# Expert weights in long runs and column halves, scan blocks taken in turn, norm tables loaded once

## The reference, cut to what matters

```python
def expert_block(args):
    xb, e = args
    return (jax.nn.silu(xb @ w_gate[e]) * (xb @ w_up[e])) @ w_down[e]

def _wkv_step(S, inp):
    r_t, w_t, k_t, v_t, a_t, b_t = inp
    sa = jnp.einsum('zbhvk,zbhk->zbhv', S, a_t)
    S = S * w_t[..., None, :] + sa[..., :, None] * b_t[..., None, :] + v_t[..., :, None] * k_t[..., None, :]
    return S, jnp.einsum('zbhvk,zbhk->zbhv', S, r_t)
```

## Time and profile before

| | us |
|---|---|
| median of 3 runs (4897.2 to 4904.73) | 4901.6 |
| span of the profiled execution | 4899.6 |
| expert stage of layer 1 / layer 2 of the second model (32 experts each), to the last down product | 729 / about 729 |
| scan, eight rounds | 1372 |
| TensorE busy | 4236.2 (86%) |
| VectorE busy | 1338.8 (27%) |
| mean granted TensorE clock | 0.789 |

### The profile page before, as it was taken

How to read it: one execution, slowest core, us unless ns; L and a number is a source line. 1 busy time by engine, 2 the same in 40 slices (tenths; PEclk the granted TensorE clock), 3 DMA queues, 4 the chain that set the end, 5 groups by cost and what they waited for, 6 DMA issues and landing times. The chain is left out here.

```text
span 4899.6 us, 68797 instructions
## 1 busy us (share of the span) xinstructions
PE 4236.2 (86%) x28873; PEld 3247.8 (66%) x28873; DVE 1338.8 (27%) x2979; ACT 474.8 (10%) x844; POOL 351.2 (7%) x471
## 2 busy tenths in 40 slices
PE   7996699989993999998497888898898885999996
PEld 6774368875542777776244776786687774777775
DVE  4533635414104000000423333423433322000001
ACT  1002210011001000000101101110110100000001
POOL 0000000000001000000001021112102100000000
PEclk9978569889695899999697555555555556999998
DMA  6732027612112899998110000000000013999995
GB/s 220 232 115 71 1 70 251 203 51 87 35 60 66 256 306 307 307 307 288 52 58 12 1 1 1 2 1 1 2 1 1 1 62 109 300 309 304 311 304 171
DMA packets 547008, 641.48 MB, mean 131 GB/s; under 512 B 26905, under 2 KB 442185, under 8 KB 546425
## 3 DMA queue, kind: packets, MB, share of 16 engines
q1 hardware_dynamic: 507460, 543.65, 34.8%
q10 hardware_dynamic: 31926, 71.73, 4.0%
q0 software_dynamic: 7424, 23.12, 1.7%
HBM read 611.67 MB, written 26.77 MB: 130 GB/s over the span
## 5 line engine op out<-in xcount | busy, mean ns | idle before, releaser
L1560 PEld LDWEIGHTS bank<-ex_xt,weights 128*128 128x128 f32 x8192 | 945.6, 196 | 52.6 <-issue 52.6
L1560 PE MATMUL bank<-ex_xt,weights 128*128 128x64 f32 x8192 | 954.4, 280 | 1.9 <-DVE ex_xt L1612 1.9
L1575 PE MATMUL bank<-weights,ex_hidden 128*64 128x512 f32 x1024 | 457.6, 600 | 4.3 <-DVE ex_hidden L1617 1.4
L394 PE MATMUL bank<-u,weights 128*128 128x272 f32 (+1 forms) x1408 | 318.0, 389 | 16.6 <-DVEq L415 16.6
L1575 PEld LDWEIGHTS bank<-weights,ex_hidden 128*64 128x64 f32 x1024 | 136.0, 138 | 278.3 <-issue 265.2
L394 PEld LDWEIGHTS bank<-u,weights 128*128 128x128 f32 x1408 | 270.3, 192 | 64.3 <-DVEq L415 17.4
L1617 DVE TENSOR_TENSOR ex_hidden<-ex_silu,bank 128x128 f32<-128x128 f32 x128 | 36.8, 288 | 906.8 <-ACT ex_silu L1593 906.8
L2333 PE MATMUL bank<-sc_xt,sc_bt 64*64 64x64 f32 x2560 | 259.4, 314 | 0.0
L2333 PEld LDWEIGHTS bank<-sc_x,sc_n 64*64 64x64 f32 x2560 | 231.9, 220 | 37.4 <-issue 37.4
L2333 PEld LDWEIGHTS bank<-sc_xt,sc_bt 64*64 64x64 f32 x2560 | 245.9, 220 | 0.0
L2333 PE MATMUL bank<-sc_x,sc_n 64*64 64x64 f32 x2560 | 239.4, 314 | 1.0 <-PEq L2253 1.0
(11 more groups left out here) (499 smaller groups left out, 4628.8 us busy)
## 6 DMA issues: line engine op xcount, KB each, us to landing
weights<-in_moe_w_gate_dram SPq DMA_DIRECT2D x128, 1024.0 KB, 5.4
weights<-in_moe_w_up_dram SPq DMA_DIRECT2D x128, 1024.0 KB, 8.0
weights<-in_moe_w_down_dram SPq DMA_DIRECT2D x128, 1024.0 KB, 8.1
ada_w<-in_ada_w_dram ACTq DMA_DIRECT2D x24, 2048.0 KB, 8.7
weights<-in_w_gate_dram SPq DMA_DIRECT2D x22, 1024.0 KB, 5.8
weights<-in_w_up_dram SPq DMA_DIRECT2D x22, 1024.0 KB, 8.2
weights<-in_w_down_dram SPq DMA_DIRECT2D x32, 704.0 KB, 6.7
weights<-in_ga_w_in_dram SPq DMA_DIRECT2D x16, 1024.0 KB, 5.6
```

The costliest lines, as they stand in the source:

```text
L394: last = nc.tensor.matmul(k.bank[b + side * NB][:, 0:N], w[:, f, c * P:(c + 1) * P], rhs[:, f, 0:N], start=(f == 0), stop=(f == DC - 1))
L1560: last = nc.tensor.matmul(k.bank[2 + q][:, o:o + SLOTS], w[:, f * 256 + c * P:f * 256 + (c + 1) * P], xt[:, s, f * SLOTS:(f + 1) * SLOTS], ...
L1575: last = nc.tensor.matmul(k.bank[4 + 2 * s + n][0:SLOTS, :], hid[:, s, f * SLOTS:(f + 1) * SLOTS], w[:, f * 512:(f + 1) * 512], start=(f = ...
```

## The change

- **Experts.** A ring of 18 slots of 1 MB (`ExpertRing`) holds three experts. SP starts the first 18 loads in the route stage. Gate and up rows are now read as "(p k)", 8 KB in one run for each partition, down rows 4 KB. For gate and up the 64 tokens are stationary and 256 columns of the weights move. The two halves of the 512 hidden columns go to partitions 0 to 63 and 64 to 127 of the same bank, so they use the left and the right half of the array. The hidden rows are then turned by two transposes and emptied by VectorE, and down uses the two halves of the array in the same way.
- **Route.** The weights' loads follow the router's small loads on SP's queue. The token rows are stored by ScalarE's queue. The overflow rows are cleared in the attention stage instead (one memset on POOL, three transfers on SP).
- **Scan.** `blocks_matmul` takes the halves in turn. Both halves of the turned copies are products with the identity, and ScalarE empties them. VectorE forms the first level of the inverse right behind each matrix.
- **Modulation.** For the first model's first layer the sums are issued behind the products of four norm stages; the head norms of the second attention are moved ahead of them. The second layer keeps `finish`.
- **Norms.** One table with both functions is asked for ahead of Ln.
- **Gate products of SwiGLU.** The eight chunks are added last to first.
- The first weights of the recurrence are loaded when expert 30 is done, no longer behind the last expert's slots.

```diff
@@ class ExpertRing @@
+    PIECES = 6
+    SLOTS = 18
+    def start(self, sp, a, l, e, j):
+        s = (self.PIECES * e + j) % self.SLOTS
+        if j < 4:
+            w = a["moe_w_gate_2" if j % 2 == 0 else "moe_w_up_2"][l, e]
+            src = w.rearrange("(p k) m -> p (k m)", k=DC)[:, (j // 2) * 2048:(j // 2) * 2048 + 2048]
+            sp.dma_start(self.slots[s], src).then_inc(self.landed[s], 16)
+        else:
+            w = a["moe_w_down_2"][l, e]
+            src = w.rearrange("(k p) m -> p k m", p=P)[:, (j - 4) * 2:(j - 4) * 2 + 2, :]
...
@@ norm_stage, and in the same way head_norm_stage, Prepare.act, scan_output @@
+            nc.scalar.preload_act_table_set("natural_log_exp_and_others")
...
+            if mods is not None:
+                mods.sums(10)
@@ gate_up_stage @@
-                        for f in range(DC):
+                        for f in reversed(range(DC)):
@@ attention_stage @@
+            pool.memset(zero[:, :], 0.0).then_inc(zeroed, 1)
...
+                    sp.dma_start(rows[n], zero[:, 0:width]).then_inc(cleared, 16)
@@ route_stage @@
-            for b in range(nov):
-                sp.dma_start(out_rows[(NE + b) * SLOTS:(NE + b + 1) * SLOTS, :], zero_row[:, :]).then_inc(cleared, 16)
+            for e in range(3):
+                for j in range(k.ring.PIECES):
+                    k.ring.start(sp, a, l, e, j)
@@ experts_stage, TensorE @@
+                    for q in range(4):
+                        f = 4 * j + q
+                        for side in range(2):
+                            w = ring.slot(e, 2 * j + side)
+                            for t in range(2):
+                                last = nc.tensor.matmul(half_cols(k.bank[2 + side], t),
                                                         xt[:, s, f * SLOTS:(f + 1) * SLOTS],
+                                                        w[:, q * 512 + t * 256:q * 512 + t * 256 + 256],
                                                         start=(f == 0), stop=(f == DC - 1))
                     last.then_inc(spent, 1)
+                if e + 1 < NE:
+                    turn(e + 1)
+                pe.wait_ge(gated, e + 1)
+                for c in range(2):
+                    last = nc.tensor.transpose(k.bank[4][:, c * P:(c + 1) * P], hid[:, s, c * P:(c + 1) * P],
+                                               k.ident[:, :])
+                last.then_inc(hturned, 1)
+                pe.wait_ge(hcopied, e + 1)
...
+                    for q in range(2):
+                        o = q * P + j * RH
+                        for n in range(2):
+                            last = nc.tensor.matmul(k.bank[6 + s][n * RH:(n + 1) * RH, :], ht[:, s, o:o + SLOTS],
+                                                    w[:, q * D + n * 512:q * D + n * 512 + 512],
+                                                    start=(j == 0 and q == 0), stop=(j == 1 and q == 1))
@@ scan_matrices @@
-                            if h == 0:
-                                last = nc.tensor.transpose(to, src, k.ident[rows, rows])
-                            else:
-
-                                last = nc.tensor.matmul(to, src, k.ident[rows, rows], start=True, stop=True)
+                            last = nc.tensor.matmul(to, src, k.ident[rows, rows], start=True, stop=True)
...
+                if kind in ("n", "nt"):
+                    x = q.x if kind == "n" else q.xt
+                    dve.wait_ge(masked, n + 1)
+                    nc.vector.tensor_tensor(chunked(x[:, z, :]), chunked(dst[:, z, :]), mask_of(q, M_LEVEL), ALU.mult)\
+                        .then_inc(vinit, 1)
+                    dve.wait_ge(vinit, n + 1)
+                    nc.vector.tensor_tensor(chunked(x[:, z, :]), chunked(x[:, z, :]), mask_of(q, M_ID), ALU.add)
+        @block.scalar
+        def _(act):
+            for n, (kind, z, ops, dst, mask) in enumerate(jobs):
+                if mask is None:
+                    act.wait_ge(made, n + 1)
+                    nc.scalar.activation(dst[:, :] if kind == "vt" else dst[:, z, :], k.bank[n % 4][:, :], ACT.Copy)\
+                        .then_inc(copied, 1)
@@ blocks_matmul @@
-    for h in HALVES:
-        rows = slice(h, h + RH)
-        for j in range(NCH):
-            t = slice(j * CH, (j + 1) * CH)
+    for j in range(NCH):
+        t = slice(j * CH, (j + 1) * CH)
+        for h in HALVES:
+            rows = slice(h, h + RH)
             last = nc.tensor.matmul(ps[rows, t], lhsT[rows, t], rhs[rows, t], start=True, stop=True)
```

More of the change, by code:

```diff
@@ L968, in share, with sums @@
         self.add(dve, r, b * self.ROUND // of, (b + 1) * self.ROUND // of)
-    def finish(self):
+    def sums(self, count):
+        nc = self.k.nc
+        for m in range(self.columns, self.columns + count):
+            for v in range(2):
+                last = nc.tensor.matmul(self.k.bank[7][:, 2 * m + v:2 * m + v + 1],
+                                        self.acc[:, v, m * P:(m + 1) * P], self.k.ones[:, 0:1], start=True, stop=True)
+        self.columns += count
+        last.then_inc(self.summed, 1)
+        self.parts += 1
@@ L1009, in ffn @@
                      side=side)
-        side.finish()
+    return side
 def param(k, name, n=1, at=0):
@@ L1571, in expert @@
-                for n in range(2):
-                    k.stream.wait(pe, seg, e, 4 + n)
-                    w = k.stream.slot(seg, 4 + n)
-                    for f in range(4):
-                        last = nc.tensor.matmul(k.bank[4 + 2 * s + n][0:SLOTS, :], hid[:, s, f * SLOTS:(f + 1) * SLOTS],
-                                                w[:, f * 512:(f + 1) * 512], start=(f == 0), stop=(f == 3))
+                if e + 1 < NE:
+                    turn(e + 1)
+                pe.wait_ge(gated, e + 1)
@@ L1602, in _, with copy @@
-            pairs(act, expert)
-            for s in range(2):
-                act.wait_ge(put[s], 16 * (NE // 2) + 16)
+            def copy(e):
+                act.wait_ge(turned, e + 1)
+                nc.scalar.activation(xt[:, e % 2, :], k.bank[e % 2][:, :], ACT.Copy).then_inc(copied, 1)
+            copy(0)
+            for e in range(NE):
+                s = e % 2
+                act.wait_ge(spent, 4 * e + 2)
+                nc.scalar.activation(act_out[:, s, :], k.bank[2][:, 0:256], ACT.Silu).then_inc(silued, 1)
+                if e + 1 < NE:
+                    copy(e + 1)
+                act.wait_ge(kept, e + 1)
+                for n in range(2):
+                    act.dma_start(out_rows[e * SLOTS:(e + 1) * SLOTS, n * 512:(n + 1) * 512],
+                                  y[n * RH:(n + 1) * RH, s, :]).then_inc(put[s], 16)
@@ L1626, in _ @@
-            copy(0, 0, 0)
-            pairs(dve, expert)
+            for e in range(NE):
+                s = e % 2
+                dve.wait_ge(silued, e + 1)
+                nc.vector.tensor_tensor(hid[:, s, :], act_out[:, s, :], k.bank[3][:, 0:256], ALU.mult)\
+                    .then_inc(gated, 1)
+                dve.wait_ge(hturned, e + 1)
+                nc.vector.tensor_copy(ht[:, s, :], k.bank[4][:, 0:256]).then_inc(hcopied, 1)
+                dve.wait_ge(spent, 4 * e + 4)
+                if e >= 2:
+                    dve.wait_ge(put[s], 32 * (e // 2))
+                nc.vector.tensor_copy(y[:, s, :], k.bank[6 + s][:, :]).then_inc(kept, 1)
@@ L1840, in moe @@
     overflow_stage(k, l, nov, rows, slots, tab, out_rows)
+    more.close()
     combine_stage(k, l, T, desti, wts, out_rows)
@@ L1947, in rwkv @@
         lw, la = sb("lw", [P, TB]), sb("la", [P, TB])
-        k.stream.hold = seg["wo"].first
         r, kx, v = (sb(n, [P, DC, TB]) for n in ("r", "k", "v"))
@@ L2252, in scan_matrices @@
     jobs.append(("vt", 0, (q.v, None), q.vt, None))
+    plain = lambda n: jobs[n][4] is None
+    turned = lambda n: sum(plain(m) for m in range(n + 1))
     with nc.Block() as block:
```

306 lines of the change are left out of this document (149 added, 157 removed).

## The result

The kernel after takes 3983.9 us (median of four runs, 3959.0 to 3994.3) against 4903.1 for the kernel before in the same job: ratio 0.8118, 95% interval 0.8092 to 0.8144. Five more runs in a later job gave 3975.6 (3966.2 to 3991.7). The forecast was 3975. The profiled run took 3987.9 us, its span is 3985.8.

A forecast was written before the change was run, and what follows sets the result against it. TensorE was taken to bound the scan and experts, with transfers close behind in experts and binding there after the change. Savings of 473 + 402 + 38 + 18 - 4 = 927 us gave 3975 us, range 3850 to 4410.

The forecast's parts named there:

- Invert, 344 us: Scan's invert: halves in turn work at once, a round goes from 92.9 to 50 us, saving 344, bounds 216 to 376.
- mostly high: Scan's invert: the clock assumed for the calls, giving 50 us a round, between 48 at high and 65.8 at low clock.
- Rival 4: Scan's invert: the clock stays low, total 4103 us; no side of its own, counted inside the forecast's 0.77.
- Matrices, 107 us: Scan's matrices: turned copies as pure products save 13.4 us a round, 107 in all, bounds 80 to 128.
- States and output, 12 and 10 us: Scan: states gains 12 us if invert leaves a high clock, bounds 0 to 16; output saves 10 in table loads.
- Experts, 402 us: Expert stages: products 12.8 us an expert, transfers then bind at 17.8; a stage takes 528 us, saving 402 in both.
- Rivals 1 and 3: Experts: array halves never work together, 4401 us, chance 0.14; or one half's load waits for the other's product, 5132, 0.04.
- Rival 2: Experts: memory gives no more than the present 297 GB/s, total 4277 us, chance 0.04.
- The smaller parts: Outside scan and experts: modulation sums save 38 us, norm table loads 18, route costs 4, the rest nothing.
- `finish` and the tables: Norm stages: first layer's sums behind norm products save 38 us; fourteen norms lose a table load each, 18 us.
- The route stage: Route: small transfers beside 18.9 MB of weights charged 4 us; 15 a layer if all scatters wait for the loads.
- The sum: Whole kernel: scan 473, experts 402, sums 38, tables 18, less 4 for route, save 927 us.

The follow-up runs named there:

- e12: Kernel after with the later third expert in layer 2, and unread products filling TensorE's gaps around the scan's round end and in invert: 3931.7 us, ratio 0.8017.
- e1: Kernel before with one edit, blocks_matmul takes the halves in turn: 4562.8 us, ratio 0.9305.
- e2: Kernel before with only scan_matrices taken from the kernel after: 4745.7 us, ratio 0.9673.
- e4: Kernel after with the same weight bytes in shorter packets, 1 KB for gate and up, 2 KB for down: 4100.9 us, ratio 0.8364.
- after_again: Kernel after, unchanged, run again in a later job: 3975.6 us, ratio 0.8106.
- e5: Kernel after without the request for the common table of Ln and Exp: 3985.4 us, ratio 0.8127.
- e6: Kernel after with the first layer's modulation sums in a stage of their own again, ahead of the mixer's norm: 4013.0 us, ratio 0.8190.
- e3: Kernel after with gate and up doing all products of one column half, then all of the other: 4034.0 us, ratio 0.8205.
- e11: Kernel after with room for one expert (6 slots instead of 18), recurrence loads starting behind the last expert: 4027.3 us, ratio 0.8211.
- e7: Kernel after with layer 2's third expert load started later, behind the load of the slot numbers: 3980.8 us, ratio 0.8117.

## Why the prediction was right

**What bounds the kernel.** Right for both stages: TensorE in the scan, and after the change the transfers in the experts, with the DMA share at 1 and every long wait ended by a load.

**Invert, 344 us.** Measured 337 over eight rounds. A round came as 53.5 us, not 50; the stage of before is 94.6 us counted from its first instruction, not 92.9. By its own items: calls 32.6 us against 27.4, since the clock falls for a while behind each gap; the preparation's products 7.2 against 5; the waits between them 8.3 against 8; start and tail 5.2 against 8. The term of the calls was mis-sized, by the words "mostly high", and e12 shows that 27 is reached once the gaps are filled. Rival 4 (1.7 us a call throughout) occurs only in the first calls behind a gap. The reason given for the high clock was half right. The halves in turn do bring the clock back, as e1 shows. But that the one-half stream sat at 0.50 in the earlier trace rows did not show that it must: it ran at 1.00 in the last round of e2.

**Matrices, 107 us.** Measured 122. The bounds of 10 to 16 a round held, the value of 13.4 was low by 1.9. Both sides of the sum were larger. In the third round the five turned copies went from 23.5 us to 6.8, a gain of 16.8 where the prediction took some 14, and the other products took 2.3 less, for which it had no term. VectorE's longer chain costs more than the 1 us that I let show: TensorE now waits 3.3 us a round for it, where behind its start it did not wait at all. Three of these waits (us in all, times, longest):

```profile
PE bank L2356 <- DVE sc_n L2375: 1.3, 1, 1.3
PE bank L2356 <- DVE sc_nt L2375: 0.9, 1, 0.9
PE bank L2356 <- DVE sc_akt L2375: 0.9, 1, 0.9
```

**States and output, 12 and 10 us.** States gained nothing: its clock was 0.70 and is 0.68, and in after invert did leave the clock high, but it fell 0.6 us into states. In e1 it ran at 0.93 and 24.1 us. The matrices stage is not the reason, since e4 runs after's scan code and has the same 24.1. Over the eight rounds that code gave states 192.0 us (e4) to 215.7 (after_again), against 213.2 before. Which of the two a run takes up, and why, is open; the 12 us lie within this spread, but the profile of after does not have them. Output gave 5 us over the eight rounds (92.5 to 87.3), and not 10, though e5 says that the load alone is worth 9 (1.2 us a round).

**Experts, 402 us.** Measured 417, 519.6 us a stage against 528. The product side was 12.45 against 12.8 us. The transfers needed 17.2 and not 17.8 us: I had added the gathers and stores as queue shares, yet 6.82 MB at the measured 396 GB/s are 17.2 with them inside. The Trainium skill's 358 GB/s a core ("DMA: Bandwidth & Descriptors", Specifications) does not bind: 396 GB/s held for 400 us. With 1 and 2 KB packets it was 348. I took the rate of a 5 us window over the 354 of the 1 KB packets. That was right by luck in the number: of that window's weight packets 813 were of 2 KB and 30 of 1 KB, and over 400 us the mix of both sizes gives 348 (e4). That 392 and more lasted is the work of the long runs.

**Rivals 1 and 3** were the real doubt, and both are out. The halves of the array do work together on the same rows (110 ns a record), and a load does not wait. Loads of 153 ns stand beside records at a pitch of 110, all on 128 rows. The rule of the Trainium skill ("TensorE: Matmul & The Clock Gate", The mechanism), that a load overlaps running products only for another row group, would have made 34 us of an expert; it took 12.45. Rival 2 (297 GB/s) was out from the start of the stage.

**The smaller parts.** `finish` and the tables were put at 38 + 18 = 56 us and gave about 44. The step that failed is that I added them up, and the 3 us that I counted for the sums' place in the norms. Up to attention there are seven norms, 9 us of loads by 1.28. Without the sums beside them (e6 against the kernel before) those loads are worth 9.9 us (548.6 against 558.5); with the sums beside them, e5 is at 524.6 and the nine others at 518.8 to 523.8, 1 to 6 us. And the sums lengthen the norms that carry them by 13.7 us where the loads are gone, while `finish` with the loads in place is worth 34 (558.5 to 524.6, e5). So each covers part of the other. Behind attention I count some 6 of 9 us for the loads, by what is left over. The 4.8 of them from combine to scan are not shown to be theirs: e5, with the loads back, has the 305.3 us of before (305.6), but e6, without the loads, has 305.7, and in all three the mean clock there is 0.835 against 0.852 in after.

The route stage cost 10.6 and not 4, all of it in layer 2, where the stage has 47 us and not 78 for the same 18.9 MB. Two items had no term. The output projection behind the scan waits 11.65 us for its start where it waited 19.07. Between the last expert and combine there are 4.9 us more. In layer 1 SP was still issuing the recurrence's loads until 2076 us, 8 us behind the last product, and the stretch to combine took 33.3 us. In e3, where SP was done ahead of the last product, it took 29.5, and in e11, where SP only then began with them, 40.0. These runs were made for other questions, but they agree that the late issues hold up the end of the stage.

**The sum.** 927 against 913.8 in the spans. Invert, states, output, the sums with the tables, and route fell short by 7, 14, 5, 12 and 7 us. Matrices and experts gave 15 each more, and what had no term 1. So that the total came within 9 us is partly luck: 45 us of shortfall stand against 31 of surplus, and the same scan code took 872.9 to 898.8 us in the profiles here. The bounds given for invert, matrices and experts all held. States went 2 us past its lower one, and route lay between the 4 us that I took and the 15 a layer that I named as the worst.

## What to carry to other kernels

When a tile uses half of the array's rows or columns, issue the halves in turn, product by product; done in blocks, most of the gain is lost. Once products are cheap, look at bytes and run length before depth: one expert of room was enough for the rate, packets of 1 KB were not. TensorE's short waits cost twice, once as the wait and once as slow products behind it, and cheap products that nobody reads in those waits were worth more here (about 40 us, e12 against after_again, less the 5 of the later third expert) than any of the small parts.

## What the runs showed of the hardware that I had not expected

- The same instructions ran the last invert at 0.50 in one kernel and at 1.00 in another, for the whole of 76.7 and 43.7 us. In these runs the stream of one-half products neither raised nor lowered the clock by itself; it went on with what it was given. In rounds 1 to 7 of e2 the clock came in high, fell behind a wait of 2.8 us and stayed at 0.50 under that stream.
- The scan of after took 898.3 us in one profile and the same code 894.6, 882.2 and 872.9 in others (e7, e6, e4). In after the second to sixth rounds agree to 0.1 us at 116.0, with the clock falling at the same place of each; in e4 they settle at 112.7. Most of the spread from 3959 to 3994 is probably of this kind. A difference of 10 us in this kernel needs the trace, stage by stage, and not the total, and even ahead of the scan the same code differs by 5 us at attention and by 10 at the scan's start.
- TensorE starts about three records of the other half ahead of their turn, both with 64x64 tiles (the single records between two calls) and with 128x64 ones (e3).
- The first gather of 64 token rows was in use 2.9 us after its issue in after and 6.7 us after it in e7, behind 6.3 MB of weights just started. A wait for four scatters of slot numbers grew from 1.5 to 5.9 us with a third expert's loads ahead. Small transfers on a chain of dependences pay here for large ones in other queues.
